# VectorE adds up a norm's squares, TensorE takes one column sum per norm

## The chip, the cores and the metric

One core of one Trainium2 chip. The metric is device time in microseconds of the whole program, lower is better. The program computes two transformer blocks one after the other on 256 tokens of width 1024 (with 16 more tokens, 272 in all, in part of the second block).

## The reference, cut to what matters

```python
def rmsnorm(x, g):
    xf = x.astype(jnp.float32)
    y = xf * lax.rsqrt(jnp.mean(xf * xf, axis=-1, keepdims=True) + EPS)
    return (y * g.astype(jnp.float32)).astype(x.dtype)

h = rmsnorm(x, g_pre_ffn1[l])                                              # norm 0
x = x + 0.5 * rmsnorm(swiglu(h, w_gu1[l], w_down1[l]), g_post_ffn1[l])     # norm 1
h = rmsnorm(x, g_pre_mix[l])                                               # norm 2
...
x = x + rmsnorm(merged @ w_out[l], g_post_mix[l])                          # norm 3
h = rmsnorm(x, g_pre_ffn2[l])                                              # norm 4
x = x + 0.5 * rmsnorm(swiglu(h, w_gu2[l], w_down2[l]), g_post_ffn2[l])     # norm 5

n = rmsnorm_2(h, g_mix[l])                                                 # norm 6, 272 tokens
...
h = h + peer(rmsnorm_2(h, g_ffn[l]), peer_wq[l], ...)                      # norm 7
h = rmsnorm_2(h, g_final)                                                  # norm 8
```

Each of the nine norms needs, for every token, the sum of 1024 squares.

## The kernel before, in words

Activations lie with features on the partitions: `x[:, k, :]` is feature tile `k` of 8 (`KT`), tokens along the free axis (`T` = 256, `L` = 272). All weights come as 550 chunks of 128 x 1024 float32 (512 KB) through a ring of six slots in SBUF, in the order of use; SP's queue loads a slot when TensorE has finished the chunk before it (`chunk_done`). ScalarE copies each chunk to a rounded high part (`hi`, L602), GpSimd or VectorE subtracts to get the low part (`lo`, L491 and L1039), and TensorE multiplies in three products, high by high, high by low and low by high (`product`, L1657 to L1660). The engines have programs written out by hand, which meet only at semaphores.

A norm goes like this. ScalarE squares each of the eight tiles (`squared_in`, L560) and raises `sq_ready`. The sum over features is a sum over partitions and over tiles, and TensorE makes both (`sum_of`, L1681 to L1690): for every tile `k` and every group of 128 tokens a matmul with the squares as stationary operand and one column of ones as moving operand, added up over `k` in one PSUM column of bank 6. That is 16 matmuls a norm, 24 in norm 6 with its 272 tokens; a float32 matmul shows as two rows in the trace. Then ScalarE takes the root (`root`, L566), VectorE the reciprocal (`inverse_root`, L980), and TensorE spreads the result over the partitions of bank 7 with two more matmuls (`spread_rstd`, L1696, shown as L1679). After norms 1, 3 and 5 six matmuls that compute nothing follow (`warm_up`, L1702).

Where the column sums stand in TensorE's program:

- Norm 0: all of them in a row, after the first two weight chunks.
- Norms 1 and 5 (end of a feed-forward block, `second` with `end`): two tiles' sums ahead of the last three products, six behind them. ScalarE squares tiles 6 and 7 when the last product has ended (`down_squares`, L585).
- Norm 3 (the mixer's output product): in pairs after every second weight chunk, the last four tiles at the end.
- Norms 2, 4 and 6 (`opening`, L1704): TensorE starts the next projection with four weight chunks side by side as soon as ScalarE has made the high part of tile 0 (`h_hi`), one step per tile, with one tile's sum behind each step; the products with the low part of the activation (L1727, they need `h_lo` of VectorE) come after all steps. The projection's results are scaled later, so only the spread needs the norm. In norm 6 two of the four chunks come eight steps later and the spread stands at step 11.
- Norms 7 and 8: all of them in a row, at the end of a stage.

VectorE's part around norms 1 and 2 is `residual(1)` (L998: eight pairs of multiply and add), then `scaled_lo` for `h_lo` (L1016), then `keep_rstd`. Norm 6 has `residual(5)`, eight `early_low` (L1011), then `norm_in` (L990).

```python
for k in range(KT):
    act_e.wait_ge(x_ready, k + 1)
    scaled_hi(2, k, "g_pre_mix")        # high part for TensorE, then the square of tile k
root(2, T)
```

## Time and profile before

| | us |
|---|---|
| three runs | 1880.05, 1878.74, 1884.32 |
| their median | 1880.05 |
| the profiled execution, as timed | 1883.23 |
| its span, first to last instruction | 1881.4 |
| TensorE busy in it | 1825.6 |
| VectorE, ScalarE, GpSimd busy | 1127.5, 846.2, 823.9 |
| mean granted TensorE clock, 1 is 2.4 GHz | 0.985 |

A row of the timeline gives start, length, engine, line of the kernel, operation, tiles, count, and in brackets how long the engine had idled just before and who ended the idling. Rows with a count of more than one merge equal instructions that follow each other; the next row can start before the end of the one above it, since instructions overlap in an engine's pipeline.

### The profile page before, as it was taken

What the parts mean: (1) busy time and instruction counts of PE and PEld (TensorE: products, weight loads), DVE (VectorE), ACT (ScalarE), POOL (GpSimd) and SP (SyncE); (2) the same over time, 40 slices, a digit from 0 to 9 for tenths busy, and PEclk for the clock granted to TensorE, in tenths of its full rate; (3) what the DMA queues carried; (4) which work ended last, traced back from release to release, by engine and by line L of the source; (5) the groups of instructions that cost most, each with busy time, mean ns of one, the idle gap of its engine ahead of it and who ended that gap; (6) DMA issues with size and microseconds to landing.
All of it is one profiled execution on the core that took longest, in us unless ns stands there. A gap on an engine that the chain in (4) does not pass through costs nothing.

```text
span 1881.4 us, 38427 instructions
## 1 busy us (share of the span) xinstructions
PE 1825.6 (97%) x14398; PEld 1756.4 (93%) x14398; DVE 1127.5 (60%) x2177; ACT 846.2 (45%) x1291; POOL 823.9 (44%) x337
## 2 busy tenths in 40 slices
PE   8999999998999999999999999999999999999998
PEld 7999997787899999986998999899999999999998
DVE  4665574675324333747662899989995555544434
ACT  4344532454454444768434454444443333334443
POOL 2666574842365666440004689500004444444442
PEclk8999999999999999999999999999999999999998
DMA  6455453521344555343454455443335555555553
GB/s 245 167 184 184 151 168 115 200 100 57 102 134 159 187 181 187 124 147 112 139 176 160 158 187 178 157 133 126 124 124 190 179 186 182 185 183 186 183 187 103
DMA packets 83906, 297.66 MB, mean 158 GB/s; under 512 B 10244, under 2 KB 12709, under 8 KB 83558
## 3 DMA queue, kind: packets, MB, share of 16 engines
q1 hardware_dynamic: 81376, 290.49, 46.6%
q10 hardware_dynamic: 2438, 5.89, 0.8%
q8 instruction: 64, 1.05, 0.2%
q14 instruction: 28, 0.23, 0.1%
HBM read 295.30 MB, written 1.05 MB: 158 GB/s over the span
## 4 chain that ended last, share of the span: by engine, by line
PE 76%; POOL 9%; DVE 7%; issue 5%; ACT 1%; DMA 1%; POOLq 0%; DVEq 0%; SPq 0%; ACTq 0%
PE ps L1658 21%; PE ps L1660 21%; PE ps L1659 21%; POOL ring_lo L491 9%; PE ps L2153 2%; PE ps L1688 1%; DVE ring_lo L1039 1%; PE ps L1864 1%; PE ps L1832 1%; PE ps L2036 1%; PE ps L1715 1%; PE ps L1716 1%; PE ps L1648 1%; DMA ring<-in_stream 1%; PE ps L1912 1%
## 5 line engine op out<-in xcount | busy, mean ns | idle before, releaser
L1660 PE MATMUL ps<-h_hi,ring_lo 128*128 128x256 f32 (+1 forms) x2432 | 687.9, 283 | 0.0
L491 POOL TENSOR_TENSOR ring_lo<-ring,peer_split 128x1024 fp32r<-128x1024 f32 x128 | 314.8, 2460 | 484.9 <-ACT peer_split L602 479.5
L1660 PEld LDWEIGHTS ps<-h_hi,ring_lo 128*128 128x128 f32 x2432 | 462.2, 190 | 0.0
L491 POOL TENSOR_TENSOR ring_lo<-ring,main_hi 128x1024 fp32r<-128x1024 f32 x113 | 282.3, 2498 | 230.2 <-ACT main_hi L602 222.6
L602 ACT ACTIVATE peer_split<-ring 128x1024 fp32r<-128x1024 f32 x256 | 270.3, 1056 | 217.1 <-PE ps L1660 217.0
L491 POOL TENSOR_TENSOR ring_lo<-ring,more_hi 128x1024 fp32r<-128x1024 f32 x87 | 225.7, 2594 | 318.4 <-ACT more_hi L602 312.8
L1658 PE MATMUL ps<-h_hi,peer_split 128*128 128x256 f32 x1024 | 292.7, 286 | 6.7 <-DVE ring_lo L1039 4.6
L1658 PE MATMUL ps<-peer_split 128*128 128x256 f32 x1024 | 289.3, 283 | 0.1
L1660 PE MATMUL ps<-peer_split,ring_lo 128*128 128x256 f32 x1024 | 288.8, 282 | 0.0
L1659 PE MATMUL ps<-h_lo,peer_split 128*128 128x256 f32 x1024 | 288.1, 281 | 0.0
L1659 PE MATMUL ps<-peer_split 128*128 128x256 f32 x1024 | 287.9, 281 | 0.0
L602 ACT ACTIVATE main_hi<-ring 128x1024 fp32r<-128x1024 f32 x159 | 167.8, 1059 | 159.3 <-DMA ring<-in_stream 108.8
L1658 PE MATMUL ps<-h_hi,main_hi 128*128 128x256 f32 (+1 forms) x776 | 222.7, 287 | 2.9 <-ACT arena L891 2.9
L1659 PE MATMUL ps<-h_lo,main_hi 128*128 128x256 f32 (+1 forms) x776 | 219.2, 283 | 0.0
L1658 PEld LDWEIGHTS ps<-h_hi,peer_split 128*128 128x128 f32 x1024 | 194.3, 190 | 8.6 <-issue 5.3
L1659 PEld LDWEIGHTS ps<-h_lo,peer_split 128*128 128x128 f32 x1024 | 194.3, 190 | 0.0
L1659 PEld LDWEIGHTS ps<-peer_split 128*128 128x128 f32 x1024 | 194.3, 190 | 0.0
L1658 PEld LDWEIGHTS ps<-peer_split 128*128 128x128 f32 x1024 | 193.3, 189 | 0.3 <-DVE ring_lo L1039 0.3
L1660 PEld LDWEIGHTS ps<-peer_split,ring_lo 128*128 128x128 f32 x1024 | 192.8, 188 | 0.0
L602 ACT ACTIVATE more_hi<-ring 128x1024 fp32r<-128x1024 f32 x109 | 115.6, 1061 | 125.2 <-DMA ring<-in_stream 122.9
L1658 PE MATMUL ps<-h_hi,more_hi 128*128 128x256 f32 (+1 forms) x552 | 159.0, 288 | 4.3 <-issue 3.9
L1039 DVE TENSOR_TENSOR ring_lo<-ring,peer_split 128x1024 fp32r<-128x1024 f32 x128 | 155.7, 1218 | 8.4 <-ACT peer_split L602 8.0
(368 smaller groups left out, 3759.0 us busy)
## 6 DMA issues: line engine op xcount, KB each, us to landing
ring<-in_stream SPq DMA_DIRECT2D x550, 512.0 KB, 3.3
arena<-in_decay ACTq DMA_DIRECT2D x1, 1536.0 KB
x<-in_x SPq DMA_DIRECT2D x4, 256.0 KB, 5.7
arena<-in_keys ACTq DMA_DIRECT2D x1, 1024.0 KB, 5.5
out<-h SPq DMA_DIRECT2D x4, 256.0 KB, 2.3
aux<-in_dft ACTq DMA_DIRECT2D x1, 816.0 KB
aux<-in_idft ACTq DMA_DIRECT2D x1, 768.0 KB
arena<-in_mask ACTq DMA_DIRECT2D x1, 768.0 KB, 5.2
```

What stands on the lines that cost most here:

```text
L491: nc.gpsimd.tensor_tensor(ring_lo[:, c % NS, :], ring[:, c % NS, :], hi_part(c).bitcast(F32), ALU.subtract).then_inc(lo_pool, 1)
L602: A(hi_part(c), ring[:, c % NS, :], ACT.Copy).then_inc(hi_ready, 1)
L1039: V.tensor_tensor(ring_lo[:, c % NS, :], ring[:, c % NS, :], hi_part(c).bitcast(F32), ALU.subtract).then_inc(lo_dve, 1)
L1648: ins = M(out, ring[:, c % NS, slot_cols + k * P:slot_cols + (k + 1) * P], rhs(k), start=(k == 0), stop=(k == nk - 1))
L1658: M(out, w_hi, parts[0], start=start, stop=False, skip_group_check=True)
L1659: M(out, w_hi, parts[1], start=False, stop=False, skip_group_check=True)
L1660: return M(out, w_lo, parts[0], start=False, stop=stop, skip_group_check=True)
L1688: ins = M(ps[0:tn, 6, t:t + 1], squares_at(n)[:, k, t0:t0 + tn], ones[:, 0:1], start=(k == 0 and t == 0), stop=(k == KT - 1), skip_group_c ...
L1715: M(out, hi_part(c)[:, k * P:(k + 1) * P], parts(k)[0], start=(k == 0 and begins[m]), stop=False, skip_group_check=True)
L1716: M(out, ring_lo[:, c % NS, k * P:(k + 1) * P], parts(k)[0], start=False, stop=False, skip_group_check=True)
L1832: ins = M(ps[0:fn, 1 + d, :], dft[0:tn, k, d, f0:f0 + fn], src[0:tn, k, :], start=(k == 0), stop=(k == 2))
L2153: ins = M(quad_bank(q)[:, m * P:(m + 1) * P], sels[q % 2][0][:, m, :], sels[q % 2][1][:, m, :], start=True, stop=True)
```

## The change

For every norm VectorE adds the eight squares tile by tile (seven additions of 128 x 256, `add_square`, each behind its `sq_ready` and behind the addition before it), and TensorE makes one column sum of the total: 2 matmuls a norm instead of 16, 3 instead of 24 in norm 6. The running sum of norms 0, 1, 3, 5, 7 and 8 lies in PSUM (bank 6, columns 240 and up), that of norms 2, 4 and 6 in SBUF; the last addition always writes to SBUF, since it becomes the stationary operand. Column sums that stood between other work now stand at one place behind it.

```diff
+        def running(n, w):
+            return squares_at(n)[:, 0, 0:w] if n in (2, 4, 6) else ps[:, 6, 512 - L:512 - L + w]
...
             def squared_in(n, k, src, w=T):
-                A(squares_at(n)[:, k, 0:w], src, ACT.Square).then_inc(sq_ready, 1)
+                A(squares_at(n)[:, k, 0:w] if k else running(n, w), src, ACT.Square).then_inc(sq_ready, 1)
...
+            def inverse_root(n, w):
+                if n != 6:
+                    inverse(n, w)
                 dve.wait_ge(rstd_spread, n + 1)
+
+            def add_square(n, k, w=T):
+                dve.wait_ge(sq_ready, KT * n + k + 1)
+                if k > 1:
+                    dve.wait_ge(sq_added, (KT - 1) * n + k - 1)
+                total = running(n, w)
+                V.tensor_tensor(total if k < KT - 1 else squares_at(n)[:, 0, 0:w], total, squares_at(n)[:, k, 0:w], ALU.add).then_inc(sq_added, 1)
+
+            def add_squares(n, after=lambda k: None, w=T):
+                for k in range(1, KT):
+                    add_square(n, k, w)
+                    after(k)
...
             lo(0)
             lo(1)
+            add_squares(0)
             keep_rstd(0)
...
             ffn(0, START["ffn1"])
+            add_squares(1)
             residual(1)
-            for k in range(KT):
+            add_squares(2, lambda k: scaled_lo(1, k - 3, "g_pre_mix") if k >= 3 else None)
+            for k in range(KT - 3, KT):
                 scaled_lo(1, k, "g_pre_mix")
...
             ffn(1, START["ffn2"])
+            add_squares(5)
             residual(5)
+            add_squares(6, w=L)
             for k in range(KT):
+                if k == KT // 2:
+                    inverse(6, L)
                 early_low(0, k, early_rgx, x[:, k, :], NORMS[6])
...
                 V.tensor_tensor(real(x, n), real(x, n), ps[:, n % 4, 0:T], ALU.add).then_inc(x_ready, 1)
+                if n > 1:
+                    add_square(7, n - 1)
+            add_square(7, KT - 1)
...
                 V.tensor_tensor(real(x, n), real(x, n), acc(n), ALU.add).then_inc(x_ready, 1)
+                if n == 3:
+                    add_square(8, 1)
+                elif n == 5:
+                    for k in (2, 3, 4):
+                        add_square(8, k)
+            for k in (5, 6, 7):
+                add_square(8, k)
...
-            def sum_of(n, k, w=T):
-                if n and k == 0:
+            def sum_of(n, w=T):
+                if n:
                     pe.wait_ge(std_ready, n)
-                pe.wait_ge(sq_ready, KT * n + k + 1)
+                pe.wait_ge(sq_added, (KT - 1) * (n + 1))
                 for t, (t0, tn) in enumerate(LT[0:2] if w == T else LT):
-                    ins = M(ps[0:tn, 6, t:t + 1], squares_at(n)[:, k, t0:t0 + tn], ones[:, 0:1], start=(k == 0 and t == 0), stop=(k == KT - 1), skip_group_check=True)
-                if k == KT - 1:
-                    ins.then_inc(ssq_ready, 1)
+                    ins = M(ps[0:tn, 6, t:t + 1], squares_at(n)[:, 0, t0:t0 + tn], ones[:, 0:1], start=(t == 0), stop=True, skip_group_check=True)
+                ins.then_inc(ssq_ready, 1)
...
-                    if n is not None and 1 <= step <= KT:
-                        sum_of(n, step - 1, w)
+                    if step == sum_at:
+                        sum_of(n, w)
                     if step == spread_at:
                         spread_rstd(n, w)
-                if n is not None and not max(late):
-                    sum_of(n, KT - 1, w)
+                if n is not None and sum_at is None:
+                    sum_of(n, w)
...
-                    early_hi, early_lo, 0, 6, (0, 0, KT, KT), L, KT + 3)
+                    early_hi, early_lo, 0, 6, (0, 0, KT, KT), L, KT + 1, KT + 6)
```

Norms 3 and 4 are treated as 1 and 2 (`add_squares(3)` ahead of `residual(3)`; `add_squares(4, ...)` with `scaled_lo` between). In norm 6 the reciprocal moves into the row of `early_low`, the sum to step 9 and the spread from step 11 to step 14.

How the programs stand. First TensorE at the end of the first feed-forward block: products of the last chunk, the sums of norm 1 (L1688, now L1731), the spread (L1679, now L1722), the warm-up (L1702, now L1744) and the start of the opening (L1715, now L1757). Before:

```order
L1660 MATMUL ps<-ffn_part,ring_lo 128x256
L1688 MATMUL ps<-square,sq 128x1 x4
L1658 MATMUL ps<-ffn_part,main_hi 128x256
L1659 MATMUL ps<-ffn_part,main_hi 128x256
L1660 MATMUL ps<-ffn_part,ring_lo 128x256
L1688 MATMUL ps<-square,sq 128x1 x12
L1679 MATMUL ps<-square,stat 128x128 x2
L1702 MATMUL ps<-square 128x128 x6
L1715 MATMUL ps<-h_hi,more_hi 128x256
L1716 MATMUL ps<-h_hi,ring_lo 128x256
```

With the change:

```order
L1701 MATMUL ps<-ffn_part,main_hi 128x256
L1702 MATMUL ps<-ffn_part,main_hi 128x256
L1703 MATMUL ps<-ffn_part,ring_lo 128x256
L1731 MATMUL ps<-square,sq 128x1 x2
L1722 MATMUL ps<-square,stat 128x128 x2
L1744 MATMUL ps<-square 128x128 x6
L1757 MATMUL ps<-h_hi,more_hi 128x256
L1758 MATMUL ps<-h_hi,ring_lo 128x256
```

Fourteen matmuls are gone from between the last products and the spread, and the two that are left come behind all products.

Second VectorE behind the residual of norm 1, where `h_lo` and the sums of norm 2 are made. Before, from the last pair of the residual on:

```order
L1004 TENSOR_TENSOR ps<-h,ps 128x256
L1009 TENSOR_TENSOR x<-x,ps 128x256 x2
L1019 SCALAR_TENSOR_TENSOR h_lo<-x,cols,h_hi 128x256 x8
L980 RECIPROCAL stat<-stat 128x2
L987 COPY rstd_out<-ps 128x256
```

With the change:

```order
L1028 TENSOR_TENSOR ps<-h,ps 128x256
L1033 TENSOR_TENSOR x<-x,ps 128x256 x2
L1000 TENSOR_TENSOR arena<-arena 128x256 x3
L1043 SCALAR_TENSOR_TENSOR h_lo<-x,cols,h_hi 128x256
L1000 TENSOR_TENSOR arena<-arena 128x256
...
L1043 SCALAR_TENSOR_TENSOR h_lo<-x,cols,h_hi 128x256 x4
L985 RECIPROCAL stat<-stat 128x2
L1011 COPY rstd_out<-ps 128x256
```

Seven additions (L1000) stand between the residual and the reciprocal, three ahead of the first `h_lo` and the others one by one between them.

Third VectorE in norm 6. Before, from the last residual addition on:

```order
L1009 TENSOR_TENSOR x<-x,ps 128x256 x2
L1014 SCALAR_TENSOR_TENSOR early_rgx_lo<-x,cols,early_rgx_hi 128x272 x8
L980 RECIPROCAL stat<-stat 128x2
L980 RECIPROCAL stat<-stat 16x1
L994 COPY rstd_out<-ps 128x272
```

With the change:

```order
L1033 TENSOR_TENSOR x<-x,ps 128x256 x2
L1000 TENSOR_TENSOR sq<-sq 128x272 x7
L1038 SCALAR_TENSOR_TENSOR early_rgx_lo<-x,cols,early_rgx_hi 128x272 x4
L985 RECIPROCAL stat<-stat 128x2
L985 RECIPROCAL stat<-stat 16x1
L1038 SCALAR_TENSOR_TENSOR early_rgx_lo<-x,cols,early_rgx_hi 128x272 x4
L1018 COPY rstd_out<-ps 128x272
```

All seven additions come ahead of the first low part, and the reciprocal stands between the fourth and the fifth.

## Rows read from the trace of the kernel before

**Rows 1.** The page: busy time, share of the span and instructions of each engine.

```profile
PE 1825.6 (97%) x14398; PEld 1756.4 (93%) x14398; DVE 1127.5 (60%) x2177; ACT 846.2 (45%) x1291; POOL 823.9 (44%) x337
```

**Rows 2.** Groups of instructions, TensorE: the column sums (busy, mean ns, idle before).

```profile
L1688 PE MATMUL ps<-square,sq 128*128 128x1 f32 (+1 forms) x208 | 24.4, 242 | 0.0
...
L1688 PE MATMUL ps<-square,arena 128*128 128x1 f32 x96 | 11.6, 236 | 0.0
```

**Rows 3.** Timeline of TensorE in norm 0 and the stage behind it.

```profile
20.47 3.63 PE L1688 MATMUL ps<-square,arena 128*128 128x1 f32 x32
...
28.41 0.61 PE L1679 MATMUL ps<-square,stat 128*128 128x128 f32 x4
...
35.45 0.55 PE L1658 MATMUL ps<-ffn_part,main_hi 128*128 128x256 f32 x1 [3.60 <-DVE ring_lo L1039]
```

**Rows 4.** Timeline of ScalarE behind the root of norm 0.

```profile
28.55 1.28 ACT L645 ACT_TABLE_LOAD   x1 [4.15 <-issue]
30.47 0.39 ACT L645 ACTIVATE arena<-ps 128x256 f32<-128x256 f32 x1 [0.64 <-DVE ps L1079]
```

**Rows 5.** Busy times by stretch: start:end, length, engines, then granted clock, DMA share, GB/s.

```profile
24.70:28.20 3.50, 3.50 (x19) 3.50 (x19) 0.00 (x0) 0.00 (x0) 0.00 (x0) 0.52 0.42 54
223.40:226.00 2.60, 2.60 (x14) 2.49 (x13) 2.53 (x8) 2.60 (x7) 0.57 (x1) 0.50 0.00 0
```

**Rows 6.** Timeline of VectorE: chained operations, a weight's low part, two additions not chained.

```profile
30.89 0.43 DVE L1081 TENSOR_TENSOR ps<-arena,ps 128x256 f32<-128x256 f32 x1 [0.45 <-ACT arena L645]
31.35 0.42 DVE L1083 CAST ffn_part<-ps 128x256 fp32r<-128x256 f32 x1
...
32.15 3.15 DVE L1039 TENSOR_TENSOR ring_lo<-ring,main_hi 128x1024 fp32r<-128x1024 f32 x1
...
228.11 0.75 DVE L1009 TENSOR_TENSOR x<-x,ps 128x256 f32<-128x256 f32 x2
```

**Rows 7.** Timeline of ScalarE in norm 1: the last two squares and the root.

```profile
219.38 0.66 ACT L560 ACTIVATE sq<-ps 128x256 f32<-128x256 f32 x2
...
221.96 0.26 ACT L566 ACTIVATE stat<-ps,small 128x2 f32<-128x2 f32 x1 [1.18 <-PE ps L1688]
```

**Rows 8.** Timeline of TensorE in norm 2: one sum between steps, and the low-part products.

```profile
227.08 0.50 PE L1688 MATMUL ps<-square,arena 128*128 128x1 f32 x4
227.44 0.36 PE L1715 MATMUL ps<-h_hi,more_hi 128*128 128x256 f32 x1
...
237.27 2.04 PE L1727 MATMUL ps<-h_lo,more_hi 128*128 128x256 f32 x16
```

**Rows 9.** Timeline of ScalarE in norm 2: high parts of tiles 0 and 1.

```profile
225.21 0.55 ACT L582 ACTIVATE h_hi<-x,cols 128x256 fp32r<-128x256 f32 x1
...
225.91 0.54 ACT L582 ACTIVATE h_hi<-x,cols 128x256 fp32r<-128x256 f32 x1
```

**Rows 10.** Timeline of ScalarE in norm 3: last squares, then the root.

```profile
551.40 0.66 ACT L560 ACTIVATE sq<-ps 128x256 f32<-128x256 f32 x2 [0.52 <-PE ps L1660]
...
553.08 0.26 ACT L566 ACTIVATE stat<-ps,small 128x2 f32<-128x2 f32 x1 [0.29 <-PE ps L1688]
```

**Rows 11.** Timeline in norm 6: last square, the spread result's copy, TensorE two chunks on.

```profile
767.22 0.45 ACT L560 ACTIVATE sq<-x 128x272 f32<-128x272 f32 x1
...
774.97 0.44 DVE L994 COPY rstd_out<-ps 128x272 f32<-128x272 f32 x1 [1.84 <-PE ps L1679]
...
787.57 0.36 PE L1658 MATMUL ps<-h_hi,more_hi 128*128 128x272 f32 x1 [0.40 <-POOL ring_lo L491]
```

**Rows 12.** Timeline of ScalarE in norm 7: the last square and the root.

```profile
1008.24 0.40 ACT L560 ACTIVATE sq<-x 128x256 f32<-128x256 f32 x1
1010.29 0.26 ACT L566 ACTIVATE stat<-ps,small 128x2 f32<-128x2 f32 x1 [1.65 <-PE ps L1688]
```

**Rows 13.** Timeline in norm 8: last residual addition on VectorE, root on ScalarE.

```profile
1869.59 0.41 DVE L1631 TENSOR_TENSOR x<-x,ps 128x256 f32<-128x256 f32 x1
...
1873.74 0.26 ACT L566 ACTIVATE stat<-ps,small 128x2 f32<-128x2 f32 x1 [3.29 <-PE ps L1688]
```

32 lines of the change are left out of this document (12 added, 20 removed).

## The prediction

> **What bounds the kernel now.** I read the busy line first: TensorE is busy for 1825.6 of 1881.4 us, every other engine for 60% or less [rows 1]. So work that leaves TensorE shortens the program wherever TensorE isn't waiting for someone. The groups say how much could leave: 304 rows of column sums, two rows a matmul, 36.0 us of busy time, with no idle time ahead of them [rows 2]. That counts overlapped rows. By its own length, a burst of 32 rows takes 3.63 us [rows 3], 0.113 us a row, so all 304 hold TensorE for some 34 us. The change leaves 38 rows of 304 (2 matmuls in eight norms, 3 in norm 6) and takes away about 30 us of TensorE. The question is how much of it stood on the path. I went through the timelines of TensorE, ScalarE and VectorE around each norm, and asked what ends last there once the sums are gone.
>
> **What VectorE pays.** Seven additions of 128 x 256 a norm. None stands in the trace in this chain, but the nearest operations do: chained through a semaphore they start 0.46 us apart (30.89 to 31.35) and last 0.42 to 0.43 us; unchained ones take 0.75 us for two, a step of 0.33 [rows 6]. I take 0.46 for chained additions and 0.33 where another operation stands between. That is 3.2 us a norm, most of it while VectorE waits for squares anyway. What counts is the tail behind the last square: one addition and four rows on TensorE in place of up to 32.
>
> **Norm 0.** VectorE is idle until the root, and the squares are ready long before TensorE finishes its second chunk, so the additions are hidden. The burst at 20.47 shrinks from 32 rows to 4, 3.2 us less [rows 3]. The granted clock stands at 0.52 in 24.7 to 28.2, right behind that burst [rows 5]; with a short burst I expect it to stay at 1.00, the 24 product rows between burst and spread then take 2.9 us and not 4.4 (24.0 to 28.41, [rows 3]). The spread comes some 4.6 us earlier, but ScalarE then sets the pace: behind the root it issues transfers for 4.15 us and loads a table for 1.28, and only then can it run L645, for which it waited another 0.64 us [rows 4]. Root 3.1 us earlier plus those 0.64: **3.7 us**; 3.0 if the clock falls all the same. TensorE's wait for the low part of chunk 4 (3.60 us, [rows 3]) hangs on that chain and moves with it.
>
> **Norms 1 and 5.** The last squares don't get earlier: ScalarE runs a weight's high part until 219.38 and then squares tiles 6 and 7, done at 220.04, while the root waits for TensorE until 221.96 [rows 7]. With the change the addition of tile 6 runs beside the last square, that of tile 7 ends near 220.7, four rows end at 221.2. **0.7 us each**, 1.4.
>
> **Norms 2 and 4.** A sum between two steps starts at 227.08 and the next product at 227.44, with a stretched gap behind it: 0.43 us for each of eight tiles [rows 8]. Without them TensorE's 96 or 64 step rows go at the pace of the low-part products, an estimated 0.117 us (2.04 us for 16 rows, less the run-out of the last, some 0.17, [rows 8]). ScalarE delivers a high part every 0.70 us (225.21, 225.91, [rows 9]); a step of norm 2 with two chunks takes 0.47 and waits for it, a step with three takes 0.71 and one with four 0.94. Laid out step by step from 225.8, when the first high part is done [rows 9], the steps end at 233.7, the one sum at 234.2, where L1727 stood at 237.27 [rows 8]: 3.1 us. VectorE's last addition ends at 232.8 (it starts at 228.8, [rows 6], two steps of 0.46, eight of 0.33 and 0.42 for itself), ahead of the sum; the last `h_lo` moves to 234.1, needed at 236. In norm 4 all four chunks run from the first step, so TensorE and not ScalarE sets every step, and by the same layout the additions end half a microsecond before the steps. **3.1 us each**, 6.2.
>
> **Norm 3.** The two pairs of sums between chunks cost 0.8 us each. ScalarE is free for the last squares at 550.88 (551.40 less its idle 0.52, [rows 10]), 0.8 us earlier with the stream; squares done at 550.8, additions at 551.4, root near 551.95 instead of 553.08. **1.1 us**.
>
> **Norm 6.** The steps are now paced by ScalarE's high parts. The last one is ready about when its square starts, 767.22 [rows 11]; its own step, two more steps of four rows and the sum end at 769.6, and five more steps lead to the spread: its copy on VectorE starts near 773.2 instead of 774.97 [rows 11]. TensorE itself gains 3.2 us, but the chunk it starts at 787.57 waits for GpSimd's low part [rows 11], which hangs on ScalarE and VectorE behind that copy. So **1.75 us**; seven additions ahead of `early_low` cost nothing, since the last low part, at some 772.4, is needed at 773.7.
>
> **Norms 7 and 8.** In norm 7 a table load holds the last square until 1008.24, the root stands at 1010.29 [rows 12]; one addition and four rows behind 1008.64 give 1009.65: **0.65 us**. In norm 8 the last residual addition starts at 1869.59 and the root at 1873.74 [rows 13]. The first four sums now stand ahead of the last two residual additions and push them back by 1.5 us; laid out, the seventh sum ends at 1872.8 and the root comes at 1873.3 to 1873.7: **0.2 us**.
>
> **Sum:** 3.7 + 1.4 + 6.2 + 1.1 + 1.75 + 0.65 + 0.2 = 15.0 us off the profiled execution's 1883.23, which is 3.2 above the median of 1880.05. I take it off the median: 1865.0 us. Downstream stages start from events that move with each norm, so nothing gives the gain back. What can be told from no change here is about 0.3%, 5.6 us.
>
> **VectorE against GpSimd.** A weight's low part on VectorE, two SBUF inputs, lasts 3.15 us at 32.15 [rows 6] beside GpSimd's; the others in that group last 0.42. Norms 2, 4 and 6 add from SBUF, and GpSimd idles in those stretches, so I charge nothing; one collision would cost up to GpSimd's share of that row, at most 2.7 us. By the Trainium skill, SBUF — State Buffer, "Who interferes with whom", a VectorE instruction with two SBUF inputs and a GpSimd one that reads SBUF exclude each other for a whole instruction. That agrees with the long row.
>
> **Rivals.** *Paced by others (16%).* In norms 2 and 4, as in norm 6, what ends last may be ScalarE or VectorE: if those two give 1.75 like norm 6 and norm 0 gives 3.0, the sum is 11.6, 1868.5 us. *Clock stays up (8%).* In the warm-up behind norm 1 the clock stands at 0.50 (14 rows in 2.60 us, [rows 5]). Shorter bursts could keep it up there and behind norms 3 and 5: half of that time and of the spread's, 1.5 us each, 1860.5 us. *Absorbed (6%).* The 550 chunks could set the pace behind each norm, so that TensorE waits for the next one; for it: TensorE does wait 0.40 us for a low part in norm 6; against it: the waits for GpSimd are short. If only norms 0, 1 and 8 keep their gain, 4.6 us, 1875.5 us. *Slower (4%).* TensorE stood busy with sums while others finished the norm; now it idles about 2.3 us before the sums of norms 1 and 5 and 1.8 in norm 3, and runs the first steps of norms 2 and 6 with gaps. If the clock then falls to 0.50 for whole openings, 96, 64 and 64 rows take at most twice their 0.117 us, 26 us more in all, and the result is 11 us slower, 1891 us. It decides from some 130 slow rows on, more than one opening. Against it: the warm-up, at 0.50 already now [rows 5], is followed by four sum rows in 0.50 us at 227.08 [rows 8], as quick as in the burst of norm 0. By the Trainium skill, TensorE: Matmul & The Clock Gate, "HAM oscillation — how this bites in real kernels", pauses between bursts let the clock drop and the next burst starts at half rate. That is the rule that speaks against the change; the trace agrees with it in the warm-up, and not behind it.
>
> **How the numbers follow.** My case 66%, and its four rivals as above. Low end 1860, where clock gains reach; high end 1873, past the paced case and half way to the absorbed one, outside which I leave some 15%. Faster by over 0.3%: 66 + 16 + 8 and a part of the absorbed case, 0.91; same 0.05; slower 0.04.
>
> **What would show it.** Right: 38 rows of column sums; L1727 of norms 2 and 4 some 3.1 us nearer to the spread of the norm before; the clock at 1.00 behind norm 0's sum; in norm 6 a wait for GpSimd of about 1.8 us where 0.40 stood; the root 1.2 us behind the last square in norms 1 and 5 (1.9 before). Wrong: clock rows of 0.50 inside the openings, sums that wait for additions there, VectorE additions of more than 0.5 us, or new waits on the stream of chunks.

## The result, and the profile after

| | before | changed |
|---|---|---|
| median, us | 1880.05 | 1867.7 |
| runs beside each other, us | 1878.74 to 1884.32 | 1865.39 to 1873.4 |
| profiled execution: timed, span | 1883.23, 1881.4 | 1873.4, 1871.6 |
| mean granted clock of TensorE in it | 0.985 | 0.981 |

The changed kernel is faster: the ratio is 0.9933, with a 95% interval of 0.9918 to 0.9949, 12.35 us at the median, where 15.0 were forecast. The result lies inside the range (1860 to 1873). The profiled execution of the changed kernel is its slowest, 5.7 us above its median, and that of the kernel before stood 3.2 above its own; so the two traces differ by 9.8 us only. Where the other 2.5 come from is one of the questions below.

The page of the changed kernel, busy times, answers to [rows 1]:

```profile
PE 1804.1 (96%) x14132; PEld 1731.1 (92%) x14132; DVE 1186.3 (63%) x2240; ACT 844.4 (45%) x1291; POOL 826.6 (44%) x337
```

TensorE has lost 266 rows of the trace (304 - 38, that is 133 matmuls of two rows) and 21.5 us of busy time (1825.6 - 1804.1), VectorE has 63 additions more. The waits of TensorE in the changed kernel (engine, line waited for, us in total, times, longest):

```profile
PE ps L1701 <- DVE ring_lo L1063: 16.2, 7, 5.5
PE ps L1731 <- DVE sq L1000: 13.1, 5, 4.0
PE ps L1701 <- POOL ring_lo L496: 4.6, 7, 2.0
```

The second row is new. L1731 is the one column sum, L1000 the additions: in five norms (1, 3, 5, 7 and 8) TensorE now stands idle until the last addition. The sums there are four rows of work each and 13.1 us of waiting in all, so where the burst was the last thing before the root, only a part of it came back.

**Norm 0**, timeline of TensorE in the changed kernel (start, length, engine, line, operation, tiles, count, idle before), answers to [rows 3]:

```profile
20.67 0.50 PE L1731 MATMUL ps<-square,arena 128*128 128x1 f32 x4
...
23.95 0.60 PE L1722 MATMUL ps<-square,stat 128*128 128x128 f32 x4
...
32.92 0.55 PE L1701 MATMUL ps<-ffn_part,main_hi 128*128 128x256 f32 x1 [5.54 <-DVE ring_lo L1063]
```

The spread comes 4.46 us earlier (28.41 before), and the first down product 2.53 (35.45 before). Between them stand ScalarE's transfers. Its timeline, which answers to [rows 4]:

```profile
21.90 1.59 ACTq L638 DMA_DIRECT2D arena<-in_zt  x1
...
26.65 1.28 ACT L650 ACT_TABLE_LOAD   x1 [5.18 <-issue]
27.94 0.38 ACT L650 ACTIVATE arena<-ps 128x256 f32<-128x256 f32 x1
```

The same eight issues took 5.18 us where they had taken 4.15. L638 alone took 1.59 (the same transfer, L633 there, 0.85 in the kernel before). That eats the 0.64 us of waiting that L645 had before, and more.

**Norm 1**, timelines of ScalarE, VectorE and TensorE in this order, answers to [rows 7]:

```profile
216.69 0.66 ACT L565 ACTIVATE sq<-ps 128x256 f32<-128x256 f32 x2
214.50 3.12 DVE L1000 TENSOR_TENSOR ps<-ps,sq 128x256 f32<-128x256 f32 x6 [1.80 <-ACT sq L565]
217.73 0.43 DVE L1000 TENSOR_TENSOR sq<-ps,sq 128x256 f32<-128x256 f32 x1
218.30 0.58 PE L1731 MATMUL ps<-square,sq 128*128 128x1 f32 x4 [2.43 <-DVE sq L1000]
218.92 0.26 ACT L571 ACTIVATE stat<-ps,small 128x2 f32<-128x2 f32 x1 [0.84 <-PE ps L1731]
```

Last square done at 217.35, last addition starting at 217.73, sum at 218.30, root at 218.92: 1.57 us, where the kernel before took 1.92. The first six additions stand in one chain of 3.12 us, 0.54 us from start to start, and it ends only at 217.62, behind the last square.

**Norms 2 and 4**, TensorE, where the sum ends the steps and the low part begins, answers to [rows 8]:

```profile
230.91 0.50 PE L1731 MATMUL ps<-square,arena 128*128 128x1 f32 x4
231.28 0.83 PE L1769 MATMUL ps<-h_lo,more_hi 128*128 128x256 f32 x5
```

From the root before it to the first low-part row it takes 12.36 us (231.28 - 218.92), where it took 15.31 (237.27 - 221.96): 2.95 less. In norm 4 11.93 where it took 15.05: 3.12 less.

**Norm 6**, VectorE and GpSimd, then TensorE two chunks on, answers to [rows 11]:

```profile
760.33 3.83 DVE L1038 SCALAR_TENSOR_TENSOR early_rgx_lo<-x,cols,early_rgx_hi 128x272 fp32r<-128x272 f32 x4
764.09 0.42 DVE L1018 COPY rstd_out<-ps 128x272 f32<-128x272 f32 x1
...
760.95 2.51 POOL L496 TENSOR_TENSOR ring_lo<-ring,main_hi 128x1024 fp32r<-128x1024 f32 x1 [7.17 <-ACT main_hi L607]
...
776.61 0.36 PE L1701 MATMUL ps<-h_hi,more_hi 128*128 128x272 f32 x1 [1.96 <-POOL ring_lo L496]
```

The wait for GpSimd is there (1.96, forecast about 1.8). But the copy starts only 4.57 us behind the root (759.52), where it had been 2.48 (774.97 - 772.49): VectorE is in the middle of four multiplications that last 3.83 us together, and beside them runs a GpSimd instruction. Three of the four take 0.47 to 0.49 us. The third, seen alone in a narrower window, takes the rest:

```profile
761.15 2.60 DVE L1038 SCALAR_TENSOR_TENSOR early_rgx_lo<-x,cols,early_rgx_hi 128x272 fp32r<-128x272 f32 x1
```

It starts 0.20 us behind GpSimd's instruction (760.95) and ends 0.29 us behind its end (763.75 against 763.46).

Going through matched events of the two traces, and taking from each the lead that it arrived with, gives what each norm earned: norm 0 2.53 us, norm 1 0.35, norm 2 2.95, norm 3 1.03, norm 4 3.12, norm 5 0.38, norm 6 0.46, norm 7 0.04, the experts' stage -0.48 and norm 8 -0.48. That is 9.9 us; the root of norm 8 comes 10.04 us earlier (1863.70 against 1873.74), so some 0.1 us is drift between the norms.

One thing stood out that no term had, the clock. Behind norm 0's sum it stays at 1.00, as forecast. Behind the longer wait (5.54 us, 3.60 before) it is at 0.50 for five microseconds (for three, 35.4 to 38.4, in the kernel before), and at 0.50 it is under norm 7's sum too. Stretches of the changed kernel (start:end, length, busy time and instructions, granted clock, DMA share, GB/s):

```profile
24.00:27.00 3.00, 3.00 (x28) 1.00 0.62 132
...
32.90:37.90 5.00, 4.98 (x23) 0.50 0.96 396
...
226.00:231.00 5.00, 5.00 (x45) 1.00 0.00 0
...
998.20:999.30 1.10, 0.98 (x4) 0.50 1.08 432
```

### The profile page after: what moved, and what is told of

The parts are those of the page before. It is cut to its first block, busy times and chain, and to the rows that moved or that the text cites. A ratio compares the mean times of both kernels' runs of the same rounds, so it can differ in the third digit from the quotient of the medians.

```text
span 1871.6 us, 38012 instructions
## 1 busy us (share of the span) xinstructions
PE 1804.1 (96%) x14132; PEld 1731.1 (92%) x14132; DVE 1186.3 (63%) x2240; ACT 844.4 (45%) x1291; POOL 826.6 (44%) x337
## 4 chain that ended last, share of the span: by engine, by line
PE 77%; POOL 9%; issue 6%; DVE 5%; ACT 2%; DMA 0%; ACTq 0%; POOLq 0%; DVEq 0%; SPq 0%
PE ps L1701 21%; PE ps L1703 21%; PE ps L1702 21%; POOL ring_lo L496 9%; PE ps L2185 2%; PE ps L1901 2%; DVE ring_lo L1063 1%; PE ps L2069 1%; PE ps L1869 1%; PE ps L1757 1%; PE ps L1758 1%; PE ps L1949 1%; PE ps L1691 1%; PE ps L2078 1%; ACT main_hi L607 1%
## 5 line engine op out<-in xcount | busy, mean ns | idle before, releaser
L1702 PE MATMUL ps<-h_lo,peer_split 128*128 128x256 f32 x1024 | 288.2, 281 | 0.0
L1702 PE MATMUL ps<-peer_split 128*128 128x256 f32 x1024 | 287.9, 281 | 0.0
L1702 PE MATMUL ps<-h_lo,main_hi 128*128 128x256 f32 (+1 forms) x776 | 220.0, 284 | 0.0
L1702 PEld LDWEIGHTS ps<-peer_split 128*128 128x128 f32 x1024 | 194.3, 190 | 0.0
L1702 PEld LDWEIGHTS ps<-h_lo,peer_split 128*128 128x128 f32 x1024 | 194.2, 190 | 0.0
```

The source lines that it names most:

```text
L1702: M(out, w_hi, parts[1], start=False, stop=False, skip_group_check=True)
```

## The experiments

Each was run five rounds beside the kernel before, and ratios are to that, with 95% intervals. Those of one group shared a chip: the two partial kernels, the one with norms 7 and 8 old and the one with the wait in norm 6; the one with matmuls ahead of the sums, the one with all constants late and the first combined one; the changed kernel's repetition, the filled waits, the constants issued early and the second combined one; the last combined one by itself.

### Do the norms' gains add up, and are they the ledger's?

The old sums were put back where a norm isn't in a list (`tile_sum` is the old function, at its old places); the second kernel has `(0, 1, 3, 5, 7, 8)` in the list:

```diff
+        ADDED = (2, 4, 6)
...
+                    if n is not None and 1 <= step <= KT:
+                        tile_sum(n, step - 1, w)
```

> The new sum in norms 2, 4 and 6 alone, the others as before: this asks whether the norms' gains add up. Additive theory: the ledger of the changed kernel against the one before gives norm 2 2.95 us, norm 4 3.12 and norm 6 0.46, so 6.5 us less than before, about 1873.5. Rival, gains overlap or are taken back by the weight stream: under 4 us. Rival, the middle column sums cost more than the gaps around them showed: over 8 us. In the trace the low-part wait of TensorE for VectorE's first tile in norms 2 and 4 stands 3 us nearer to the end of the work before it than in the kernel before, and norm 0's and norm 1's roots stand where they stood before.

> The new sum in norms 0, 1, 3, 5, 7 and 8, norms 2, 4 and 6 as before. Additive theory: norm 0 2.5 us, norm 1 0.35, norm 3 1.0, norm 5 0.4, norm 7 0.0, norm 8 -0.5, so 3.8 us less than before, about 1876.3; together with the run on norms 2, 4 and 6 this must come to the 10.3 us that the two traces differ by (12.35 by the medians of the runs). If the two parts sum to clearly less, the gains are not additive; if clearly more, one of them hides the other in the full change.

Measured: norms 2, 4 and 6 alone 1878.38 us, ratio 0.9982 (0.9971 to 0.9993); the other six alone 1879.17, 0.9983 (0.9967 to 0.9999). By the medians that is 2 and 1 us, far less than 6.5 and 3.8, and the rival in the first expectation, under 4 us, would hold. The eleven and twelve executions of these kernels spread over 8.5 and 14.9 us, though, and their traces say something else. TensorE's first low-part rows of norms 2 and 4 in the first kernel, then that of norm 2 in the second:

```profile
234.76 0.48 PE L1794 MATMUL ps<-h_lo,more_hi 128*128 128x256 f32 x2
563.15 0.36 PE L1794 MATMUL ps<-h_lo,more_hi 128*128 128x256 f32 x1
```

```profile
234.42 0.40 PE L1791 MATMUL ps<-h_lo,more_hi 128*128 128x256 f32 x2
```

The roots ahead of them start at 221.84, 551.23 and 218.06. So the distances are these, beside the other kernels' (us):

| distance | before | 2, 4, 6 alone | the rest alone | changed, two traces |
|---|---|---|---|---|
| root 0 to first down product | 11.31 | 11.31 | 11.45 | 11.72, 11.39 |
| root 1 to norm 2's low part | 15.31 | 12.92 | 16.36 | 12.36, 12.36 |
| root 3 to norm 4's low part | 15.05 | 11.92 | 15.10 | 11.93, 11.94 |
| root 5 to the chunk behind norm 6 | 29.15 | 28.77 | 30.70 | 28.69, 28.60 |
| root 7 to root 8 | 863.45 | 862.65 | 865.21 | 864.41, 865.12 |

The gain of an opening goes with its new sum: 12 to 13 where the sum is new, 15 to 16 where it is old. What is left within a group is the clock: behind norm 1 it is at 0.50 until 223 in the changed kernel's first trace, which takes 12.36, and until 228 in the one with 2, 4 and 6 alone, which takes 12.92. (The 30.70 holds 1.52 us in which ScalarE waited for a chunk of the stream, once.) So the ledger's terms stand in the traces, and the medians have something on top of them.

### What lies on top: the clock

For 175 timed executions, all but the first five of the kernel before and one of it that took 5784.65 us, the mean granted clock of each is on record. A line through them with one level for each kernel and chip falls by 1.40 us for each 0.001 of clock (standard error 0.07), and leaves 1.7 us of scatter. The kernel before alone, 72 executions from 1874.7 to 1888.0 us, gives 1.24. At a clock of 0.984, where the kernel before mostly is, the line gives 1881.1 for it, 1875.4 for norms 2, 4 and 6 alone, 1877.6 for the rest alone, and 1868.6 for the changed kernel (each of the last three to some 1 or 1.5 us). That is 5.7, 3.5 and 12.5 us: the parts are where the ledger has them, 6.5 and 3.8, and the whole is 3.3 us more than their sum of 9.2 (standard error 0.9), which stays open.

This correction takes a kernel's clock as if it had nothing to do with the edit, and that isn't shown. The eleven executions with norms 2, 4 and 6 alone have a mean clock of 0.9825 (standard error 0.0006), the 26 of the kernel before beside them 0.9843 (0.0002). That is more than chance gives, and at 1.40 us for 0.001 it is most of the 4 us by which the median falls short of the 5.7. So this kernel has its gain in the openings and seems to lose much of it in clock elsewhere; that the gains add is shown for the distances, not for the times.

To see where the clock goes, the changed kernel itself ran once more.

> The changed kernel itself once more, beside the next three on one chip, so that they can be compared with it and so that there is a second trace of it. Clock theory of the spread: over the runs so far the time falls by 1.4 us for each 0.001 of mean granted clock, and the kernels' traces show stretches at 0.50 that begin behind waits of 2 to 5 us and are not the same ones from trace to trace. So the second trace differs from the first where, and only where, one has a stretch at 0.50 and the other not; the median lies between 1867.7 and 1872.4, the runs from about 1864 to 1876. Rival, other work moved (transfers, waits): stages differ by over 1 us at equal clock.

Measured: 1870.82 us (1867.68 to 1873.48), ratio 0.9941 (0.9928 to 0.9954), inside what was expected. With the five runs above, ten executions have a median of 1869.4. Two traces of one and the same program, the product behind one and the same wait, its row of TensorE's timeline and the busy times of the stretch that it begins. First trace:

```profile
1019.22 0.38 PE L1701 MATMUL ps<-h_hi,main_hi 128*128 128x256 f32 x1 [2.87 <-ACT arena L896]
```

```profile
1019.20:1024.20 5.00, 4.98 (x42) 1.00 0.55 188
```

Second trace:

```profile
1018.61 0.58 PE L1701 MATMUL ps<-h_hi,main_hi 128*128 128x256 f32 x1 [2.76 <-ACT arena L896]
```

```profile
1018.60:1023.60 5.00, 4.99 (x23) 0.50 0.43 168
```

The wait is the same, 2.9 and 2.8 us, but behind the one 42 instructions run in five microseconds at full clock, behind the other 23 at half. The other places that differ: 495 to 500 is at 0.66 in the first trace and 1.00 in the second; 1205 to 1210 likewise; behind the 4.3 us wait of the second feed-forward stage, from 566, both fall, the second for longer. The Trainium skill, TensorE: Matmul & The Clock Gate, "Part 1: The HAM clock gate (the "warmup" mystery)", says that the number of slow matmuls at a kernel's start differs from run to run; in these two traces it does so a thousand microseconds in as well.

Summed over half-microsecond windows, TensorE's busy time multiplied by the missing share of the clock comes to 24.0 us in the kernel before, 29.5 and 29.6 in the two traces of the changed one, 22.2 in the fastest trace with norms 7 and 8 left old (below). That is 5.5 us more than before in the traces at hand, and about 1 us more on average by the line (mean clock 0.9833 in ten executions against 0.9841 in 72), which the standard error of the ten, 0.0005 or 0.7 us, hardly tells from nothing. So the change pays at most a small price to the clock, and the lottery of one execution is several times as large.

### Norms 7 and 8

```diff
+        ADDED = (0, 1, 2, 3, 4, 5, 6)
```

> The changed kernel with norms 7 and 8 summed as before (twenty or forty small column sums between x tiles rather than adds and one late sum). Half-clock theory: in the changed kernel TensorE stands idle 2.4 and 4.0 us ahead of these sums, they run at a granted clock of 0.50 and take 0.98 us instead of about 0.5, and the adds' last step stands between the last square and the sum. Without it 0.5 us of norm 8 and none of norm 7 come back: 0.5 us less than the changed kernel. Rival: it is VectorE's last add alone (0.43 us and its wait), then the same 0.5 comes back, but the four last sum rows of norm 7 run at 0.50 here too. Rival, my ledger's -0.5 at norm 8 was chance: no difference.

Measured: 1873.28 us (1864.49 to 1879.81), 0.9961 (0.9946 to 0.9975); at equal clock 1870.7, no gain that the times can show. By the traces root 7 to root 8 takes 862.85 us. Of the other traces with the clock down in the same two places of that stretch, the kernel before and the one with 2, 4 and 6 alone (old sums) have 863.45 and 862.65, the changed kernel 864.41. That is 1.0 to 1.8 us more, where I had a gain of 0.85 for norms 7 and 8. (A fourth trace with the old sums, the first combined kernel's below, has 866.66, with the clock down in a third place, 1024 to 1030.)

Smaller distances part this. From root 7 to the first residual addition of norm 8 the three traces with the old sums take 856.83, 856.49 and 856.60 us, the changed kernel 857.31 with the clock down 2 us longer. From that addition to root 8 they take 6.63, 6.16 and 6.25, the new sum 6.70 in five traces and 7.10 in the two in which its four rows ran at half clock. The old sum at full clock, in the last two kernels of this document, takes 5.61 and 5.60. So at like clock the new sum of norm 8 costs 0.5 to 1.1 us, and the rest of the 1.0 to 1.8 goes with the clock in the experts' stage. The 0.5 us that was expected from taking it back is there in the trace, 0.85 (7.10 against 6.25).

Norm 7 is another matter. The root stands 1.65 us behind the last square in the kernel before, 1.62 in the changed one, whose sum runs at half clock, and 1.22 in three kernels whose new sum ran at full clock (the ones of the next experiments with GpSimd held back, with all constants late and with filled waits; the first of them here):

```profile
997.47 0.58 PE L1732 MATMUL ps<-square,sq 128*128 128x1 f32 x4 [2.45 <-DVE sq L1001]
```

The gain forecast for norm 7 is there, 0.4 of 0.65 us, when the clock is up, and gone when it is down.

Timeline of VectorE and TensorE at the end of the changed kernel, which answers to [rows 13]:

```profile
1861.04 0.96 DVE L1000 TENSOR_TENSOR ps<-ps,sq 128x256 f32<-128x256 f32 x2
1862.11 0.42 DVE L1000 TENSOR_TENSOR sq<-ps,sq 128x256 f32<-128x256 f32 x1
...
1862.68 0.98 PE L1731 MATMUL ps<-square,sq 128*128 128x1 f32 x4 [3.98 <-DVE sq L1000]
```

VectorE's queue now holds the last residual additions and seven square additions in one row, and TensorE, which used to sum beside them, idles for 3.98 us and then needs 0.98 for four rows in this trace.

> The changed kernel with eight 128x128 matmuls on the identity, into a bank that nothing reads then, ahead of TensorE's wait for the last add in norms 1, 3, 5, 7 and 8. They compute nothing that is used. Half-clock theory: they keep TensorE from standing idle, so the four sum rows of norms 7 and 8 run at 1.00 and take 0.5 us where they took 0.98: 0.5 us less for each, 1 us in all, and the spread 0.9 where it took 1.2: another 0.3 each. Rival: eight matmuls of 0.05 to 0.1 us each end long before the adds do and TensorE idles again, the granted clock stays at 0.50, and the time is that of the changed kernel.

```diff
+                for _ in range(8 if n in (1, 3, 5, 7, 8) else 0):
+                    M(ps[:, 7, 0:P], ident, ident, start=True, stop=True)
                 pe.wait_ge(sq_added, (KT - 1) * (n + 1))
```

Measured: 1872.12 us (1868.52 to 1875.57), 0.995 (0.9931 to 0.9968). The sums do run at full rate (0.61 us in norm 7, 0.60 in norm 8, where 0.98 stood), and the mean clock is up at 0.984 to 0.989, but the time isn't down. I take it that the matmuls lift the clock of stretches in which TensorE has nothing to do; no run tests that. Without matmuls ahead of it the sum took 0.58 us as well, in norm 7 in three other kernels' traces and in norm 8 in five. The 0.4 us of a half-clock sum is real and too small to show in the times.

### Norm 6: who stands in VectorE's way

```diff
             root(6, L)
+            act_e.wait_ge(early_lo, KT)
             hi_to(START["rgx"] + 5)
```

> The changed kernel with one wait more: in norm 6 ScalarE holds the high part of rgx's sixth tile, and with it GpSimd's low part, until VectorE has multiplied its eight low parts by the gain. Collision theory: in the changed kernel GpSimd's low part, 2.51 us, runs beside VectorE's early multiplications, each engine slowing the other; VectorE's four rows that meet it take 3.83 us where eight took 3.39 before, and the copy of the spread comes at 2.07 us behind the spread's start where 0.97 stood before. With the two apart, the copy comes about 1.1 us earlier and the time falls by up to 1.1 us, by less if GpSimd's tile, now started 1 to 2 us later, is what TensorE then waits for (it waited 1.96 us for it in the changed kernel). Rival: the tile GpSimd makes is the bound, then the wait moves to it and the time rises by about 1 us.

Measured: 1872.4 us, 0.9955 (0.994 to 0.997); at equal clock 1869.8, the changed kernel's within the error. The trace, VectorE and GpSimd, then TensorE:

```profile
759.09 1.71 DVE L1039 SCALAR_TENSOR_TENSOR early_rgx_lo<-x,cols,early_rgx_hi 128x272 fp32r<-128x272 f32 x4
761.74 0.44 DVE L1019 COPY rstd_out<-ps 128x272 f32<-128x272 f32 x1 [0.94 <-PE ps L1723]
...
761.96 2.41 POOL L496 TENSOR_TENSOR ring_lo<-ring,main_hi 128x1024 fp32r<-128x1024 f32 x1 [9.48 <-ACT main_hi L607]
...
774.28 0.38 PE L1702 MATMUL ps<-h_hi,more_hi 128*128 128x272 f32 x1 [1.84 <-POOL ring_lo L496]
```

and the stretch behind that wait:

```profile
774.00:778.00 4.00, 3.71 (x17) 0.57 0.29 115
```

The same four multiplications take 1.71 us without GpSimd beside them and 3.83 with it. Root to copy is 3.47 instead of 4.57, and root 6 to the chunk behind the wait 16.01 instead of 17.09: the collision theory, 1.1 us, to a tenth. Yet root 6 to root 7 takes 239.82, as in the changed kernel (239.77): behind the wait of 1.84 us the clock fell here, and not in the changed kernel behind 1.96. A kernel without the added wait speaks for the gain: in the trace with matmuls ahead of the sums (section before) the clock falls in the same place (0.51 over 775 to 778.5), and root 6 to root 7 takes 240.84. At like clock the added wait is worth 1.0 us at root 7 too, one trace against one, and here the fallen clock took it back.

### The first down product: ScalarE's issues

Three kernels try the step that norm 0's gain got stuck in. First, all eight issues far behind the root, behind the second silu; then the first five ahead of the root.

> The changed kernel with eight issues of constant transfers on ScalarE moved from behind the first root to behind the second silu. Two of the changed kernel's rows say that ScalarE's issues stand between the root and its first high parts: its load of a function table waits 5.18 us for them where it was 4.15 us before, and TensorE's wait for chunk 4's low part fell by 2.53 us only where the root came 2.94 earlier. If that step paces the first product, moving eight issues off it takes 2 to 4 us from that wait, and the time falls by about 2 us; if the low parts are paced by VectorE (rival), nothing falls behind the first product, and the time is that of the changed kernel within 0.5 us.

Measured: 1876.86 us (1872.89 to 1882.03), 0.9979 (0.9965 to 0.9993): worse than the changed kernel, where 2 us less were expected. Root 0 to the first down product is 9.78 us where 11.3 to 11.7 stood in six traces with the new sum of norm 0 and all eight issues behind its root, so the issues do stand in the way. But the last constant then comes late, and TensorE waits for it:

```profile
48.56 0.71 PE L1831 MATMUL ps<-arena 33*64 33x272 f32 x1 [5.67 <-DMA aux<-in_idft]
```

> Three edits together: norms 7 and 8 summed as before, the extra wait of norm 6, and the eight constant transfers issued later. If each is worth what its own theory says and they add, 0.5 + 1.1 + 2 us less than the changed kernel: about 1864. If only some of them hold, it falls by their sum.

Measured: 1876.51 us (1871.2 to 1882.3), 0.9977 (0.9963 to 0.9992), with the same wait (5.2 us), where 1864 was expected. One part lost more than the other two earned. Then a version with five of the eight issues moved:

```diff
             hi_to(5)
-            root(0, T)
             act_e.dma_start(x[:, :, 0:NM], meta_d).then_inc(loaded_const, 16)
...
             act_e.dma_start(w3[0:FW + 1, :], w3_d).then_inc(loaded_const, 16)
+            root(0, T)
             act_e.dma_start(decay, decay_d).then_inc(loaded_const, 16)
```

> The changed kernel with the first five issues of constant transfers on ScalarE ahead of the first root and the last three behind it, all eight still in their order. Theory: the root waits about 2 us for TensorE's sum anyway, so the five (2.3 us in the kernel before, 3.6 in the changed one) are mostly hidden there, the table load behind the root starts 2 us sooner, TensorE's wait ahead of the first down product ends 1 to 2 us sooner, and, as the last constants land no later than in the changed kernel, nothing waits for them (where all eight were moved far behind, TensorE waited 5.67 us for the last one): 1 to 2 us less than the changed kernel. Rival: the five delay the root by as much as they save behind it: no difference.

Measured: 1871.81 us (1870.34 to 1874.0), 0.9955 (0.9942 to 0.9967). ScalarE and TensorE:

```profile
22.72 1.28 ACT L650 ACT_TABLE_LOAD   x1 [1.09 <-issue]
...
31.14 0.36 PE L1701 MATMUL ps<-ffn_part,main_hi 128*128 128x256 f32 x1 [3.60 <-DVE ring_lo L1063]
```

Again 9.78 us from the root (21.36), nothing waits for a constant, and root 0 to root 1 takes 195.84 where the changed kernel has 197.55 to 197.72: 1.7 us, as expected. The five executions don't show it (1871.8 against 1870.8 beside it); their spread is as large as the gain.

### Filling the waits

> The changed kernel with 128x128 matmuls on the identity, into columns of a bank that nothing reads, in five of TensorE's longest waits that end in a product: 12 ahead of the first low-part wait of the first feed-forward stage (5.5 us), 10 ahead of that of the second (4.3), 5 ahead of the sixth rgx tile (2.0), 8 behind wq's opening (2.9), 10 ahead of the first down product of the experts (3.3). They compute nothing that is used. Clock theory: behind each such wait the products run at 0.50 for a while in some or all traces and lose 1.7 to 3.1 us there; with the engine kept at work they run at 1.00, each matmul takes about 0.27 us and all end inside the wait, the mean clock rises to about 0.99 and the time falls by 4 to 8 us. Rival, the matmuls themselves meet a fallen clock (0.55 us each) and end behind the wait: no gain, or up to 3 us slower. Rival, the clock falls there in spite of them: same time, same clock.

```diff
                 pe.wait_ge(act_ready, f * FT + 1)
+                warm_up(10 if f else 12)
                 second(0, 0, True, False)
...
+            warm_up(10)
             second(0, begin=True)
```

Measured: 1873.56 us (1867.66 to 1876.41), 0.9952 (0.9935 to 0.9969). No gain, where 4 to 8 us were expected, and three findings in the trace. Stretches behind the second stage's wait, behind the first stage's, and behind the wait after that:

```profile
569.60:574.60 5.00, 5.00 (x42) 1.00 0.24 79
32.20:37.20 5.00, 5.00 (x42) 1.00 1.00 402
53.50:58.50 5.00, 5.00 (x24) 0.50 0.01 2
```

The filled waits do what they should: 1.00 where both traces of the changed kernel were down, and root 3 to root 5 takes 200.41 us where the two traces of the changed kernel had 201.73 and 202.39, 1.3 and 2 us less. But behind the first stage the products then run ahead of the weights. The next wait for a low part was 0.89 us in the changed kernel (at 54.41) and is

```profile
53.45 0.55 PE L1701 MATMUL ps<-ffn_part,main_hi 128*128 128x256 f32 x1 [3.12 <-DVE ring_lo L1063]
```

and behind that one the clock fell instead. And ten of the matmuls stood where TensorE doesn't wait (ahead of the first down product of the experts): each costs 0.245 us, 2.5 in all. The wait of 3.31 us is one place earlier.

### Two combined versions

> All that the traces so far speak for: norms 7 and 8 summed as before (root 7 to root 8 takes 1.1 us less so in four traces of either kind, clock's losses subtracted), the wait that keeps GpSimd and VectorE apart in norm 6 (1.1 us), the matmuls that fill five waits (4 to 8 us by the clock theory) and five constant issues ahead of the first root (1 to 2 us). If they add, 7 to 12 us less than the changed kernel, about 1861; if the filled waits do nothing, 3 us less.

Measured: 1867.67 us (1864.27 to 1875.66), 0.9936 (0.9917 to 0.9955). That is 3.2 us below the changed kernel beside it, where 7 to 12 were expected. 2.5 of what is missing are the ten matmuls that stand where TensorE doesn't wait. The next version moves them; the edit, against this one:

```diff
                 ins.then_inc(ew_turned, 1)
+            warm_up(10)
...
-            warm_up(10)
             second(0, begin=True)
```

> The last combined version with one filling put right: its ten matmuls in the experts' stage stood ahead of the first down product, where TensorE doesn't wait, so they cost 2.5 us; the 3.3 us wait is ahead of the first gate tile behind the three transposes, and they now stand there. Everything else as before: norms 7 and 8 summed the old way, GpSimd and VectorE kept apart in norm 6, four waits filled, five constant issues ahead of the first root. Clock theory: 2.5 us for the matmuls and up to 1.7 for the stretch at 0.50 behind that wait, so 2.5 to 4 us less than the last version's 1867.7: about 1864. Rival, that stage's time is set elsewhere: root 7 to root 8 stays at 865.

Measured: 1866.12 us (1862.88 to 1867.95), 0.9919 (0.9903 to 0.9935). Root 7 to root 8 takes 861.45 us where the version before it took 864.98: 3.5, inside the 2.5 to 4 expected; the whole is 2 us above the 1864 expected. Against the changed kernel's ten executions the median is 3.3 us less and all six lie below 1868; the two ratios' intervals overlap a little and the chips differ, so that it beats the kernel before is clear, that it beats the changed one is likely. At equal clock the line gives it 1870.1, no less than the changed kernel's 1868.6: what it has over that one goes with its higher mean clock (0.987 against 0.983), which the filled waits were meant to give. The refilled wait, in TensorE's timeline, and the stretch behind it:

```profile
1194.00 0.82 PE L2221 MATMUL ps<-square,arena 128*128 128x128 f32 x6
1194.66 2.40 PE L1767 MATMUL ps<-square 128*128 128x128 f32 x20
1198.13 0.36 PE L1710 MATMUL ps<-h_hi,peer_split 128*128 128x256 f32 x1 [1.08 <-DVE ring_lo L1072]
```

```profile
1198.00:1203.00 5.00, 4.87 (x41) 1.00 0.12 29
```

## Why the prediction was nearly right, point by point

- **What counts is the tail behind the last square.** Right. Some 30 us of sums left TensorE (266 rows at 0.113 us; 21.5 of it shows as less busy time, since other rows ran longer at the lower clock of this trace) and 12 came off the time. Where sums stood between steps that TensorE itself paced, they came back whole; where they ran while others finished the norm, they turned into the 13.1 us of waiting for L1000.
- **What VectorE pays.** Right in the length, 0.42 to 0.44 us each, and too low in the step: 0.54 apart in a chain (six in 3.12 us, less 0.43 for the last, over five), where I took 0.46 from two other operations.
- **Norms 2 and 4, 3.1 us each.** 2.95 and 3.12. The step-by-step layout from ScalarE's and TensorE's paces holds. The rival that others pace these openings falls.
- **Norm 3, 1.1 us.** 1.03, in part by luck: the root came 1.48 us behind the last square and not 1.15 (the same chain as below), and the squares came some 0.2 us earlier than laid out.
- **Norms 1 and 5, 0.7 us each.** 0.35 and 0.38, half. The mis-sized term is the tail: "the addition of tile 6 runs beside the last square, that of tile 7 ends near 220.7". The chain of additions was itself still at work when the last square ended, since its steps are 0.54 and not 0.46 us (six of them end at 217.62 in norm 1, the last square at 217.35), and the sum took 0.58: 1.57 us and not 1.2.
- **Norm 0, 3.7 us.** 2.5. The root came 2.94 earlier and the clock stayed up, as forecast. The term that failed is "behind the root it issues transfers for 4.15 us": I moved a duration as if it were fixed, and the issues took 5.18 and 4.85 in two traces. It is no chance of two traces: in all seven with the new sum of norm 0 and all eight issues behind its root, at 19.9 to 21.3, they took 4.44 to 5.18, one of them (zt) 1.03 to 1.62; in the two with the old sum, root at 24.14 and 23.14, 4.15 and 4.16, with 0.85 for zt, as where they were issued much earlier or later. What they meet around 21 us no run shows. Three kernels that take issues from behind the root show that this is the step, 1.6 to 1.9 us of it. And the clock, which I had gained behind the burst, is down for longer behind the wait that took the burst's place (0.50 over 32.9 to 37.9; before, 0.50 over 35.4 to 38.4).
- **Norm 6, 1.75 us.** 0.46 to 0.55. The step that failed is in "VectorE against GpSimd": "so I charge nothing; one collision would cost up to GpSimd's share of that row". I looked for collisions with the added additions only. It came to one by shift: the earlier root releases GpSimd's low part earlier, while VectorE, which had been through with `early_low` by then, still had four tiles to do, because seven additions stood ahead of them. Keeping the two apart gave 1.1 us back, which makes 1.5. By the Trainium skill, SBUF — State Buffer, "Who interferes with whom", the two exclude each other for a whole instruction; the one multiplication of 2.60 us, which started just behind GpSimd's 2.51 us instruction and ended just behind it, agrees.
- **Norms 7 and 8, 0.65 and 0.2 us.** Norm 7 gave 0.4 us where the clock was up and nothing in the changed kernel's traces, where it was down at the sum and into the opening. Norm 8 cost 0.5 to 1.1 us at like clock. The step that failed there is "push them back by 1.5 us; laid out, the seventh sum ends at 1872.8": the additions on VectorE and the wait for the last of them outweigh the burst that they replace, and the root was 1.17 us behind the last addition (1862.53 to 1863.70, 0.98 of it a sum at half clock) and not up to 0.9. That an idle TensorE pays with its clock stood only under the rival "slower", for whole openings, and not in these two terms.
- **Clock stays up (8%).** Falls in the warm-up; there it is 0.50 as before. **Slower (4%).** Its place, the openings of norms 2 and 6, is at 1.00 (226 to 231). Its mechanism exists all the same, at waits of 2 to 5 us, and what it cost in the changed kernel is about 1 us on average, hardly clear of nothing. In four other kernels' traces the low clock of the warm-up reached into norm 2's opening, to between 226.5 and 228, and that opening took 12.7 to 12.9 us and not 12.4.
- **Absorbed (6%).** Not in the changed kernel. But the kernels that speed up the first stage further meet it at once: the wait for the next low part is 1.95 us with the issues early and 3.12 with the waits filled, where 0.89 stood.
- **The sum.** 9.9 us by the ledger, 12.5 at equal clock, 12.35 by the first medians, 11.8 by the medians of all ten and all 72 executions, 15.0 forecast. The result is nearer to the forecast than the terms are: norms 0, 1, 5, 6, 7 and 8 together had 7.7 us forecast and 2.8 in the ledger with the experts' stage, and only the openings and norm 3 came as laid out. That the ledger is 2.5 us short of the line isn't settled: the two traces' clocks differ, and the correction by half-microsecond windows counts idle filling (the warm-up) as loss, so it can't be used to a microsecond.

## What to carry to other kernels

Taking work off the busiest engine is worth what ends last at each place: lay out the other engines' events there, and price the gap that the removed work leaves too, both for the clock behind it and for what starts earlier because of it and may now meet someone on a shared port. Where executions of one kernel spread by 10 us, compare distances between matched events in traces and executions at equal clock before believing that an edit of 1 to 3 us did or didn't work. Matmuls that keep the engine at work are worth placing only inside a wait that the trace shows, and only where what follows isn't waiting for the stream anyway.

## What was not expected of the hardware

- The same program at the same wait (2.87 and 2.76 us) ran on at 1.00 in one execution and at 0.50 in the next; each 0.001 of mean clock goes with 1.40 us, and that is most of the spread of 10 us and more between executions.
- Four VectorE multiplications of 128 x 272 with two SBUF tensors took 3.83 us beside one GpSimd instruction and 1.71 without, and all of the difference is in one of them, which took 2.60; GpSimd's own took 2.51 against 2.41.
- The eight transfer issues of ScalarE took 4.15 us behind a root at 24.14 and 4.85 and 5.18 behind one 3 us earlier; one of them (zt) 0.85, 1.11 and 1.59.
- Holding back the constant transfers by some 9 us made TensorE wait 5.67 us, and root 0 to root 1 took 201.83 us and not 197.6: their landing was the next bound, and no row of the kernel before showed it.
